# Copying the second quarter of the expert rows behind the state-space tile loads

## The chip, the cores and the metric

The kernel runs on one core of a Trainium2 chip. The metric is the device time of one execution in microseconds (us). The core has five engines that run side by side: TensorE (PE: matrix products and transposes), VectorE (DVE), ScalarE (ACT), GpSimd (POOL) and SyncE (SP), which here only issues DMA transfers. Every engine works through its own instructions in order and waits on semaphores. The transfers that SP issues are listed as queue q1 in the profile and are moved by 16 DMA engines.

## The reference

One token block of 512 positions (and 256 context positions) with 1024 channels goes through two models. The first has two layers, the second ends in a product-key expert layer:

```python
def first_block(...):                      # two layers, l = 0 and 1
    # l = 0: latent attention and retention, joined by w_out
    o_c, o_l = mla_retention_mixer(h_c, h_l, ...)
    x = x + mod_l[:, 2] * o_l
    x = x + mod_l[:, 5] * squared_relu_mlp(h_l, mlp_w1[l], mlp_w2[l])
    # l = 1: a diagonal state-space model in both directions, then a gated unit
    o_c, o_l = s5_mixer(h_c, h_l, p_f, p_b, d_skip, w_glu, need_ctx)
    ...                                    # and the second perceptron

def peer_ffn(h, wq, subkeys, u_tab, v_tab):     # u_tab, v_tab: 16384 rows of 1024 floats each
    ...                                    # 128 rows of each table are chosen for every token
    act = jax.nn.gelu(jnp.einsum('phkd,pd->phk', u_tab[ib], tb)) * gb
    return jnp.einsum('phk,phkd->pd', act, v_tab[ib])
```

All numbers are 32-bit floats.

## The kernel before

The program is one long list of instructions for each engine. Its stages follow one another on TensorE: attention (to about 330 us), retention with its input and output projections (to 680 us), the first perceptron (to 1352 us), the state-space layer (1370 to 1585 us), its gated unit and the second perceptron (to about 1885 us), and then the second model with the expert rows (to 3895 us).

**The expert tables.** For the second half of the tokens the kernel gathers the u row and the v row of an expert in one indirect transfer, from a DRAM tensor `expert_rows` whose row is the two rows side by side (8 KB). That tensor is made during the run from the two tables: `keep_rows(sp, a, which)` (L1218) issues one transfer from DRAM to DRAM for each table, 512 rows of 4 KB, 2048 KB each; in `expert_rows` such a row of 4 KB stands 8 KB behind the last. Rows 0 to 8191 are copied during the first perceptron, two transfers behind each weight block and its two kept pieces (L959, L968 and L977). Rows 8192 to 12287 are copied in one run of 16 transfers behind the load of `w_out` in the retention stage (L1298 and L1299). The last 4096 are copied in the second perceptron, one transfer behind each weight block (L970 and L979). The first gather waits until all 64 are done (L1528), at about 3217 us.

**The state-space stage.** Its matrices were made by GpSimd during the first perceptron and put in DRAM (`s5_store`). Eight tiles i = 0 to 7 are worked through, and for each SP issues three loads: F (`tile_F`, 1024 KB, L1312) and the table (`tile_tab`, 768 KB, L1313), which count on the same semaphore `s5_F`, and E (`tile_E`, 1024 KB, L1316). Each has two buffers. F and the table of tile i wait until TensorE has done `mm1` of tile i-2 and VectorE has turned its states; E of tile i waits for `y` of tile i-2 (L1315). Behind E of tiles 1, 3 and 5 the four weight blocks `xkv` of the memory attention are loaded (2048 KB each: two, one, one; L1318). SP issues in this order, so F of tile i+1 stands behind E of tile i and, for odd i, behind a weight block.

TensorE's order is that of `s5_order()`: for tile i the products `y` (L3152 and L3157), then for tile i+2 the transposes `ta` (L3102), `fa` (L3120) and `tb` (L3113), then `yb` (L3166) of tile i and `fi0` (L3131), `fb` (L3120 again), `mm0` (L3142), `fi1` of tile i+1, one piece of the memory's projections (L3074 or L3081), and `mm1`. `fa` waits for F and the table of its tile, `mm0` for E. ScalarE copies what `fa` makes (L1793) and what `tb` makes (L1797 and L1798) out of the banks, in this order; `fi0` waits for these.

**Behind the stage.** When all pieces of the memory's projection are out of their banks, SP stores them (`kv_kept`, L1322), waits until that has landed, loads the two weight blocks `ada1_4` and then the gated unit's weights. TensorE's next work (L745) needs `ada1_4`.

Of the kernel before, what the change touches and what calls it, by code (L numbers as in the profile page):

```python
# [558 lines left out]
def build(nc, I, consts, out):  # L559

    ctx = ExitStack()
    with ctx:
# [5 lines left out]
        def S(name):  # L568

            if name not in sems:  # L570
                sems[name] = ctx.enter_context(nc.semaphore(name))
            return sems[name]
# [34 lines left out]
        def filled(eng, t, extra=0):  # L607

            eng.wait_ge(S(f"bank{bank_of[t]}_full"), use_of[t] + 1 + extra)
            return ps[bank_of[t]]  # L610
# [34 lines left out]
        def load_block(eng, b, src, extra=0):  # L645


            before = [c for c in range(b) if slot_of[c] == slot_of[b]] or [c for c in range(b) if (slot_of[b], slot_of[c]) in ((NSLOT, 2), (NSLOT + 1, 3))]
            if before:
                filled(eng, last_use[before[-1]], extra)  # L650
            n = 1
            for s in src.shape[1:]:
                n *= s
            dst = ring_part[slot_of[b]][0:src.shape[0], 0:n]
            if len(src.shape) == 3:
                dst = dst.rearrange("p (a b) -> p a b", a=src.shape[1])
            if len(src.shape) == 4:
                dst = dst.rearrange("p (a b c) -> p a b c", a=src.shape[1], b=src.shape[2])
            eng.dma_start(dst, src).then_inc(S(f"weights{slot_of[b]}"), 16)
# [52 lines left out]
        for _i, _vec in enumerate((VEC_A, VEC_B, VEC_C)):  # L712
            _n = sum(v.shape[0] for _, v in _vec)
            vec_rows.append((at(6 * D + _i * P, P), _vec, _n))
            vec_cols.append(sb(f"vec_cols{_i}", [P, _n]))
            _r = 0
            for _name, _v in _vec:
                col_of[_name] = (_i, _r)
                _r += _v.shape[0]

        def col(name, j=0, n=1):

            i, r = col_of[name]
            return vec_cols[i][:, r + j:r + j + n]

        ACT_VECS = [n for _, v, _ in vec_rows for n, _ in v][::2]
        SMALL_LOADS = sum(len(v) for _, v, _ in vec_rows) + 2 - len(ACT_VECS)
        dve_step, act_step, pool_step = Steps("dve_done"), Steps("act_done"), Steps("pool_done")
        silu_c = sb("silu_c", [P, KD, 2])
# [5 lines left out]
        def ada_load(sp, b, l, q):  # L735
            for j in range(2):
                load_block(sp, b + j, ada_w[l][:, :, (2 * q + j) * 512:(2 * q + j + 1) * 512])
# [480 lines left out]
        def keep_rows(sp, a, which):  # L1218

            for w in which:  # L1220
                sp.dma_start(expert_rows[bass.ds(a, 512), w * D:(w + 1) * D], (I["peer_u_2"], I["peer_v_2"])[w][0][bass.ds(a, 512), :])\
                  .then_inc(S("rows_kept"), 16)
# [51 lines left out]
        def _(sp):  # L1274
# [20 lines left out]
                             I["s5_w_glu"][0].rearrange("(k p) n -> p k n", p=P)[:, :, 256 * b:256 * b + 256]).then_inc(S("weights_kept"), 16)  # L1295
            for j in range(2):
                load_block(sp, block0["w_out"] + j, I["w_out"][0].rearrange("(k p) n -> p k n", p=P)[:, :, j * 512:(j + 1) * 512])
            for j in range(8):  # L1298
                keep_rows(sp, 8192 + 512 * j, (0, 1))  # L1299
            ada_load(sp, block0["ada1_2"], 1, 2)  # L1300
            mlp_loads(sp, 0)
            ada_load(sp, block0["ada1_3"], 1, 3)
# [5 lines left out]
            for i in range(S5_TILES):  # L1308
                if i >= 2:
                    filled(sp, ticket0[f"s5_mm1{i - 2}"] + 1)  # L1310
                    sp.wait_ge(S("s5_turned"), 2 * (i - 2) + 2)
                sp.dma_start(tile_F[i % 2], s5_store[i, :, 0:2048]).then_inc(S(f"s5_F{i % 2}"), 16)  # L1312
                sp.dma_start(tile_tab[i % 2], s5_store[i, :, 4096:5632]).then_inc(S(f"s5_F{i % 2}"), 16)  # L1313
                if i >= 2:
                    filled(sp, ticket0[f"s5_y{i - 2}"] + 1)  # L1315
                sp.dma_start(tile_E[i % 2], s5_store[i, :, 2048:4096]).then_inc(S(f"s5_E{i % 2}"), 16)  # L1316
                for j in {1: (0, 1), 3: (2,), 5: (3,)}.get(i, ()):
                    load_block(sp, block0["xkv"] + j, w_kv[:, :, 512 * j:512 * j + 512])  # L1318
            for n in range(8):
# [2200 lines left out]
```

## Time and profile before

| | us |
|---|---|
| median of 3 runs | 3904.86 (3902.64 to 3905.81) |
| the profiled execution | 3898.42, its span 3895.5 |
| PE busy in the span | 3408.8 (88%) |
| DVE, ACT, POOL busy | 1983.0 (51%), 935.9 (24%), 1110.5 (29%) |
| copies into `expert_rows` from SP | 64 transfers of 2048 KB, 20.4 (u) and 21.9 (v) from issue to landing (median) |
| mean granted clock of TensorE | 0.94 |

The profile gives, for one execution, the busy time of the engines, the chain of work that ended last (each step followed back to what released it), groups of instructions with what they waited for, and for a transfer the time from its issue to its landing. TensorE's granted clock is 1.00 (2.4 GHz) or 0.50 (1.2 GHz) of full speed.

### The profile page before, as it was taken

How to read it: one execution, taken by the hardware profiler on the slowest of the kernel's cores; microseconds unless marked ns; L12 is line 12 of the kernel's file. 1: busy time of each engine (PE TensorE's matmuls, PEld its weight loads, DVE VectorE, ACT ScalarE, POOL GpSimd, SP SyncE). 2: the span in 40 equal slices, each digit the busy share in tenths (PEclk: the TensorE clock that was granted, in tenths of full speed). 3: DMA queues.
4: the chain of work that ended last, by engine and by line, in shares of the span. 5: the costliest groups of instructions: out<-in, count | busy, mean ns of one | idle time of the engine just before them, and what ended most of it. 6: DMA issues, size and time to landing. Idle time of an engine off the chain costs nothing.

```text
span 3895.5 us, 47385 instructions
## 1 busy us (share of the span) xinstructions
PE 3408.8 (88%) x17855; PEld 2216.6 (57%) x17855; DVE 1983.0 (51%) x4548; ACT 935.9 (24%) x2125; POOL 1110.5 (29%) x1281
## 2 busy tenths in 40 slices
PE   7999999999999999999989999998687897555655
PEld 4566545555555578788878887765455543111111
DVE  3341263733222388311363257787787436676764
ACT  4352033200000122110342221125423222212212
POOL 1000003262233100000000136654657663333432
PEclk9999999999999999999999999999798999877687
DMA  4439985997785333699322369998879999999998
GB/s 181 149 132 311 322 284 126 317 315 228 246 250 162 124 141 123 219 374 329 121 87 76 125 264 404 413 399 311 307 240 372 392 396 392 421 421 392 421 421 343
DMA packets 337275, 1076.47 MB, mean 276 GB/s; under 512 B 22728, under 2 KB 101012, under 8 KB 292148
## 3 DMA queue, kind: packets, MB, share of 16 engines
q1 hardware_dynamic: 222688, 508.04, 38.2%
q0 software_dynamic: 113968, 565.16, 37.0%
q8 instruction: 125, 2.05, 0.2%
q10 hardware_dynamic: 420, 0.62, 0.1%
q14 instruction: 74, 0.61, 0.0%
HBM read 1045.43 MB, written 236.98 MB: 329 GB/s over the span
## 4 chain that ended last, share of the span: by engine, by line
PE 66%; DVE 15%; DMA 10%; ACT 5%; issue 3%; another core or an unknown queue 1%; POOL 0%; SPq 0%; DVEq 0%; ACTq 0%; POOLq 0%
PE bank L1004 23%; PE bank L3248 9%; PE bank L3474 5%; DMA arena<-expert_rows,arena 4%; DVE ring L2757 4%; DMA ring<-expert_rows,arena 4%; PE bank L2981 3%; PE bank L3215 3%; PE bank L3047 2%; PE bank L3178 1%; DVE arena L2757 1%; DVE arena L2651 1%; PE bank L2857 1%; DMA arena<-in_peer_v,arena 1%; PE bank L2973 1%
## 5 line engine op out<-in xcount | busy, mean ns | idle before, releaser
L3474 PE MATMUL bank<-arena 64*64 64x512 f32 x2520 | 399.4, 704 | 133.0 <-ACT arena L2032 116.3
L1004 PE MATMUL bank<-hT,ring 128*128 128x256 f32 (+1 forms) x1536 | 443.7, 451 | 2.2 <-ACT hT L888 1.7
L1004 PE MATMUL bank<-arena,ring 128*128 128x256 f32 (+1 forms) x1536 | 442.1, 450 | 0.0
L1004 PEld LDWEIGHTS bank<-hT,ring 128*128 128x128 f32 x1536 | 291.1, 190 | 153.5 <-issue 120.3
L3248 PE MATMUL bank<-hT,ring 128*128 128x256 f32 x1536 | 360.8, 393 | 19.8 <-DVE hT L2473 13.1
L1004 PEld LDWEIGHTS bank<-arena,ring 128*128 128x128 f32 x1536 | 291.8, 190 | 148.9 <-issue 121.5
L3474 PE MATMUL bank<-ring,arena 64*64 64x512 f32 x1256 | 239.0, 785 | 138.2 <-ACT arena L2032 137.7
L3248 PEld LDWEIGHTS bank<-hT,ring 128*128 128x128 f32 x1536 | 297.8, 197 | 85.1 <-issue 37.1
L1520 POOL DMA_INDIRECT ring<-in_peer_u,arena x256 | 277.4, 1084 | 208.8 <-DVE ring L2757 94.6
L1562 POOL DMA_INDIRECT arena<-in_peer_v,arena x240 | 276.6, 1153 | 180.8 <-PE bank L3474 62.5
L2757 DVE SCALAR_TENSOR_TENSOR ring<-ring,xT 128x1024 f32<-128x1024 f32 x256 | 309.0, 1220 | 22.8 <-DMA ring<-in_peer_u,arena 17.4
L3474 PEld LDWEIGHTS bank<-arena 64*64 64x64 f32 x2520 | 100.9, 150 | 348.2 <-ACT arena L2032 169.7
L2032 ACT ACTIVATE arena<-arena,rstd 128x64 f32<-128x64 f32 x472 | 141.3, 339 | 421.5 <-DVE rstd L2803 398.5
L2757 DVE SCALAR_TENSOR_TENSOR ring<-ring,bank 128x1024 f32<-128x1024 f32 x141 | 171.7, 1220 | 103.7 <-DMA ring<-expert_rows,arena 101.9
L3474 PEld LDWEIGHTS bank<-ring,arena 64*64 64x64 f32 x1256 | 57.2, 160 | 284.3 <-ACT arena L2032 215.4
L1036 DVE SCALAR_TENSOR_TENSOR xT<-bank,modT,xT 128x512 f32<-128x512 f32 (+1 forms) x96 | 54.8, 573 | 316.6 <-PE bank L1004 316.4
L1016 ACT ACTIVATE arena<-bank 128x512 f32<-128x512 f32 (+1 forms) x96 | 43.5, 454 | 712.5 <-PE bank L1004 712.4
L799 POOL TENSOR_TENSOR hT<-hT 128x256 f32<-128x256 f32 (+1 forms) x30 | 34.7, 1156 | 581.5 <-ACT hT L1937 261.1
L1539 POOL DMA_INDIRECT ring<-expert_rows,arena x141 | 133.5, 947 | 232.6 <-PE bank L3474 200.6
L1028 DVE TENSOR_TENSOR arena<-arena 128x512 f32<-128x512 f32 (+1 forms) x96 | 55.7, 589 | 276.5 <-ACT arena L1016 275.7
L2757 DVE SCALAR_TENSOR_TENSOR arena<-arena,bank 128x1024 f32<-128x1024 f32 x115 | 140.2, 1220 | 75.0 <-DMA arena<-expert_rows,arena 73.5
L1539 POOL DMA_INDIRECT arena<-expert_rows,arena x115 | 108.7, 945 | 179.0 <-PE bank L3474 154.2
(601 smaller groups left out, 5348.0 us busy)
## 6 DMA issues: line engine op xcount, KB each, us to landing
expert_rows<-in_peer_u SPq DMA_DIRECT2D x32, 2048.0 KB, 20.4
expert_rows<-in_peer_v SPq DMA_DIRECT2D x32, 2048.0 KB, 21.9
ring<-in_mlp_w SPq DMA_DIRECT2D x32, 2048.0 KB, 11.2
ring<-in_ada_w SPq DMA_DIRECT2D x24, 2048.0 KB, 10.5
late_weights<-in_mlp_w SPq DMA_DIRECT2D x32, 1024.0 KB, 14.4
ring<-late_weights SPq DMA_DIRECT2D x32, 1024.0 KB
ring<-weights_kept SPq DMA_DIRECT2D x32, 1024.0 KB
s_store<-arena POOLq DMA_DIRECT2D x8, 2816.0 KB, 9.8
```

Of the source, the lines that this page charges most:

```text
L1004: last = pe.matmul(bank[:, 0:hi - lo], w[:, k, m * P:(m + 1) * P], x[:, k, lo:hi], start=(k == 0), stop=(k == 7))
L1028: dve.tensor_tensor(hid[:, m, lo:hi], hid[:, m, lo:hi], hid[:, m, lo:hi], ALU.mult)\
L1520: pool.indirect_dma_start(u_row[u % ERING], None, I["peer_u_2"][0], bass.IndirectOffsetOnAxis(idxs[:, u // EXPERTS, u % EXPERTS:u % EXPERT ...
L1539: pool.indirect_dma_start(both_rows[i % F_SLOTS], None, expert_rows, bass.IndirectOffsetOnAxis(idxs[:, u // EXPERTS, u % EXPERTS:u % EXPER ...
L1562: pool.indirect_dma_start(v_row[v_slot(v)], None, I["peer_v_2"][0], bass.IndirectOffsetOnAxis(idxs[:, v // EXPERTS, v % EXPERTS:v % EXPERT ...
L2032: act.activation(diag[:, d % V_SLOTS, :], eye2, ACT.Copy, scale=acts[:, d % (AGROUP * ACT_GROUPS):d % (AGROUP * ACT_GROUPS) + 1]).then_inc ...
L2757: dve.scalar_tensor_tensor(row, row, 1.0, h_tok[u // EXPERTS], ALU.mult, ALU.mult, accum_out=dots[:, u % 64:u % 64 + 1]).then_inc(S("u_use ...
L2981: last = pe.matmul(bank[:, 0:hi - lo], w[:, k, m * P:(m + 1) * P], hT[:, k, lo:hi], start=(k == 0), stop=(k == KD - 1))
L3047: last = pe.matmul(bank[:, 0:hi - lo], w[:, k, m * P:(m + 1) * P], mixT[:, k, lo:hi], start=(k == 0), stop=(k == 7))
L3215: last = pe.matmul(bank[:, 0:HALF], w[:, k, n % 2 * P:n % 2 * P + P], y, start=(k == 0), stop=(k == KD - 1))
L3248: last = pe.matmul(bank[:, first:first + HALF], w[:, k, c:c + P], y, start=(k == 0), stop=(k == KD - 1))
L3474: last = pe.matmul(banks[2 * r + n][QUADS[r if y == 0 else 1 - r], :], diag[QUADS[r], (v + y) % V_SLOTS, :], v_part(v + y)[QUADS[r], 512 * ...
```

## The change

The run of 16 copies leaves the retention stage. In the state-space stage each tile's loads are followed by the two copies of 512 rows. Same transfers, same bytes, the same semaphore; nothing is added to a wait.

```diff
@@ sync engine, behind the loads of w_out
             for j in range(2):
                 load_block(sp, block0["w_out"] + j, I["w_out"][0].rearrange("(k p) n -> p k n", p=P)[:, :, j * 512:(j + 1) * 512])
-            for j in range(8):
-                keep_rows(sp, 8192 + 512 * j, (0, 1))
             ada_load(sp, block0["ada1_2"], 1, 2)
@@ sync engine, loop over the state-space tiles
                 if i >= 2:
                     filled(sp, ticket0[f"s5_y{i - 2}"] + 1)
                 sp.dma_start(tile_E[i % 2], s5_store[i, :, 2048:4096]).then_inc(S(f"s5_E{i % 2}"), 16)
+                keep_rows(sp, 8192 + 512 * i, (0, 1))
                 for j in {1: (0, 1), 3: (2,), 5: (3,)}.get(i, ()):
                     load_block(sp, block0["xkv"] + j, w_kv[:, :, 512 * j:512 * j + 512])
```

SyncE in the retention stage, the change against the kernel before. The rows with a minus are the first two of 16 copies of `keep_rows`; `in_ada_w` is the load of `ada1_2`:

```order
 L1294 DMA gate_weights<-in_s_w_glu 1024x1x256 x8
 L659 DMA ring<-in_w_out 128x8x512 x2
-L1221 DMA expert_rows<-in_peer_u 512x1024
-L1221 DMA expert_rows<-in_peer_v 512x1024
...
 L659 DMA ring<-in_ada_w 128x8x512 x2
 L659 DMA ring<-in_mlp_w 128x8x512
```

The load of `ada1_2` now stands directly behind `w_out`.

SyncE in the state-space stage before, tiles 3 and 4: F, the table and E of tile 3, the third `xkv` block, then tile 4.

```order
L1312 DMA arena<-s5_store 128x2048
L1313 DMA arena<-s5_store 128x1536
L1316 DMA arena<-s5_store 128x2048
L659 DMA ring<-in_xattn_wkv_2 128x8x512
L1312 DMA arena<-s5_store 128x2048
L1313 DMA arena<-s5_store 128x1536
L1316 DMA arena<-s5_store 128x2048
```

The same place after the change:

```order
L1310 DMA arena<-s5_store 128x2048
L1311 DMA arena<-s5_store 128x1536
L1314 DMA arena<-s5_store 128x2048
L1221 DMA expert_rows<-in_peer_u_2 512x1024
L1221 DMA expert_rows<-in_peer_v_2 512x1024
L659 DMA ring<-in_xattn_wkv_2 128x8x512
L1310 DMA arena<-s5_store 128x2048
L1311 DMA arena<-s5_store 128x1536
L1314 DMA arena<-s5_store 128x2048
```

Two copies of 2048 KB now stand between E of a tile and everything that SP issues next: for tile 3 that is the weight block and then F and the table of tile 4.

## Rows read from the trace of the kernel before

**Rows 1.** Chain of work that ended last, whole span: start, duration, what.

```profile
465.59 41.29 PE bank L2981 x128
692.05 660.04 PE bank L1004 x2044
```

**Rows 2.** SyncE's timeline, retention stage: start, duration, what was issued.

```profile
442.09 3.60 SPq L1221 DMA_DIRECT2D expert_rows<-in_peer_u  x1
544.22 19.75 SPq L659 DMA_DIRECT2D ring<-in_ada_w  x2
```

**Rows 3.** TensorE's timeline, state-space stage; brackets: idle before, and its releaser.

```profile
1447.36 1.04 PE L3120 MATMUL bank<-ident,arena 128*128 128x128 f32 x8
1473.09 1.04 PE L3120 MATMUL bank<-ident,arena 128*128 128x128 f32 x8
1474.44 0.85 PE L3113 MATMUL bank<-ident,arena 96*128 96x96 f32 x8 [0.31 <-ACT arena L1785]
1478.92 2.06 PE L3142 MATMUL bank<-arena 64*128 64x128 f32 x32
1524.56 1.04 PE L3120 MATMUL bank<-ident,arena 128*128 128x128 f32 x8
```

**Rows 4.** SyncE's timeline, state-space stage.

```profile
1421.73 0.43 SPq L1313 DMA_DIRECT2D arena<-s_store  x1
1448.00 0.65 SPq L1313 DMA_DIRECT2D arena<-s_store  x1
1472.28 0.32 SPq L1316 DMA_DIRECT2D arena<-s_store  x1
1499.47 0.76 SPq L1313 DMA_DIRECT2D arena<-s_store  x1
```

**Rows 5.** Issue to landing (last number, us): tables of tiles 3, 4, 6.

```profile
arena<-s_store SPq DMA_DIRECT2D x1, 768.0 KB, 8.4
...
arena<-s_store SPq DMA_DIRECT2D x1, 768.0 KB, 14.4
...
arena<-s_store SPq DMA_DIRECT2D x1, 768.0 KB, 14.3
```

**Rows 6.** Windows, perceptron one: engines' busy us, clock, DMA share, GB/s.

```profile
940.00:952.00 12.00, 12.00 (x37) 6.81 (x36) 3.06 (x6) 0.00 (x0) 0.00 (x0) 1.00 1.00 351
952.00:968.00 16.00, 16.00 (x50) 9.20 (x49) 8.43 (x13) 0.00 (x0) 0.00 (x0) 1.00 1.00 259
```

**Rows 7.** SyncE's timeline, perceptron two.

```profile
1776.21 0.38 SPq L659 DMA_DIRECT2D ring<-in_mlp_w  x1
1776.85 0.83 SPq L1221 DMA_DIRECT2D expert_rows<-in_peer_v  x1
```

**Rows 8.** Issue to landing of those two.

```profile
ring<-in_mlp_w SPq DMA_DIRECT2D x1, 2048.0 KB, 10.1
expert_rows<-in_peer_v SPq DMA_DIRECT2D x1, 2048.0 KB, 14.7
```

**Rows 9.** SyncE's timeline, end of the state-space stage.

```profile
1549.47 0.32 SPq L1316 DMA_DIRECT2D arena<-s_store  x1
1567.26 0.32 SPq L1322 DMA_DIRECT2D kv_kept<-ring  x1
1575.40 1.01 SPq L659 DMA_DIRECT2D ring<-in_ada_w  x2
```

**Rows 10.** TensorE's timeline, first work behind the stage.

```profile
1589.87 4.90 PE L745 MATMUL bank<-ring,silu_c 128*2 128x256 f32 x64 [4.42 <-issue]
```

**Rows 11.** Issue to landing: E of tile 7, and `kv_kept`.

```profile
arena<-s_store SPq DMA_DIRECT2D x1, 1024.0 KB, 5.3
...
kv_kept<-ring SPq DMA_DIRECT2D x1, 2048.0 KB, 8.1
```

**Rows 12.** Windows around 1370 us, columns as in rows 6.

```profile
1366.40:1370.60 4.20, 0.03 (x1) 0.00 (x0) 3.63 (x8) 4.20 (x9) 0.44 (x2) 1.00 1.05 388
1370.60:1374.00 3.40, 3.04 (x15) 2.98 (x16) 2.65 (x4) 2.00 (x5) 0.61 (x2) 0.50 0.94 343
```

## The prediction

> **What bounds the kernel now.** I read the chain of work that ended last first. In the retention stage and in the first perceptron it is TensorE without a break: one piece of 41.29 us while the 16 copies run, and later one of 660.04 us [rows 1]. SP issues the first copy at 442.09 and gets to the next load, `ada1_2`, at 544.22 [rows 2]. So the copies fill the DMA queue for some 100 us, but no TensorE, VectorE or ScalarE work of the chain waits for a transfer there. In the state-space stage the chain is TensorE and ScalarE in turn, with a period of 25.73 us: `fa` of tile 3 starts at 1447.36, that of tile 4 at 1473.09 [rows 3]. TensorE is idle there for fractions of a microsecond only, so whatever makes `fa` or `mm0` late is added to the end.
>
> The reader should look next at the distance between a load's landing and its use. The table of tile 4 was issued at 1448.00 [rows 4] and landed 14.4 us later [rows 5], at 1462.4; `fa` of tile 4 needs it at 1473.09, 10.7 us later. The table of tile 6: 1499.47 + 14.3 = 1513.8, needed at 1524.56 [rows 3 to 5], 10.8 us. These two stand behind an `xkv` block. The table of tile 3 has no such block ahead: 1421.73 + 8.4 = 1430.1, needed at 1447.36, 17.3 us.
>
> **What goes.** The 16 copies leave the retention stage. Loads behind them on SP come earlier: `ada1_2` is needed only for the perceptron, 100 us and more after it was issued [rows 1, 2], and what follows it waits for free slots. GpSimd's loads have the queue more to themselves, but its products are wanted only at the state-space stage. I take the gain as zero; as the chain has no transfer in this stretch, I see no bound below it except a microsecond or so.
>
> **What comes.** Eight pairs of copies, one behind E of each tile. A later load on the queue is moved back by what a pair takes (p). Three rows give p:
> - Pairs in a long full queue: (544.22 - 442.09) / 16 = 6.38 us for one copy, p = 12.8 [rows 2].
> - A pair in a short burst behind a weight block and its kept pieces, with the queue empty before: between 952 and 968 us 16 us at 259 GB/s, which is 4.14 MB, the pair's 4.19 MB, against 351 GB/s in the 12 us before [rows 6]. p = 16.0.
> - A single copy behind a single weight block: block landed at 1776.21 + 10.1 = 1786.3, copy at 1776.85 + 14.7 = 1791.6 [rows 7, 8], 5.2 us. Two of these would be p = 10.5.
>
> I take 16.0, because the state-space pairs are also u and v back to back, in short bursts behind loads, with an empty queue between. The ends are 10.5 and, as nothing excludes a slower one, some 18.
>
> Tiles 0 and 1: their loads and copies are issued as soon as the perceptron's last block is in use, before the stage begins; two pairs, 32 us, fit ahead of it, and the first `xkv` blocks wait for slots anyway. Hidden. Tile 3: 17.3 us of distance against p = 16.0. Hidden by 1.3 us. Tile 5 has no weight block ahead either, and 5 us more once tile 4 was late. Hidden. E of tile 4 is issued at 1472.28 [rows 4], behind a table that then has just landed; it needs about 3 us of transfer more and is wanted at 1478.92 plus the delay [rows 3]. Hidden.
>
> Tile 4: the pair of tile 3 goes ahead of `xkv`, F and the table. Landing 1462.4 + 16.0 = 1478.4, 5.3 us after `fa` wanted to start. Of these 0.3 us are covered, since `tb` waits 0.31 us for ScalarE anyway [rows 3]: **+5.0 us**. Tile 6 the same way: 1513.8 + 16.0 - 1524.56 = 5.2, less 0.3: **+4.9 us**. The two add up, since SP issues tile 6's loads when `y` of tile 3 is done, which is late by the first delay.
>
> The stage's end: E of tile 7 lands at 1549.47 + 5.3 = 1554.8, and the last pair goes behind it to 1570.8. `kv_kept` is issued at 1567.26 and takes 8.1 us alone [rows 9, 11]; SP waits for it, then loads `ada1_4` at 1575.40, and TensorE stands idle for it for 4.42 us until 1589.87 [rows 9, 10]. So this string of transfers is already on the path. `kv_kept` would move bytes from about 1569; the pair holds them to about 1570.5: **+1.7 us**, and nothing if p is under 14.3.
>
> The clock: after a gap of 4.2 us without TensorE work the granted clock was 0.50 for the next 3.4 us [rows 12]. Such a piece costs at most 1.7 us of TensorE time (an estimate, half of 3.4). Two gaps of about 5 us may bring none, one or two. I take one: **+1.7 us**.
>
> Sum: 5.0 + 4.9 + 1.7 + 1.7 = 13.3 us. The profiled execution was 3898.42 (its span 3895.5), 6.4 under the median 3904.86; I add the sum to the median: **3918 us**, or about 3909 for the span.
>
> As a function of p the sum is 2 (p - 11.0) + (p - 14.3, if positive) + the clock: 3.6 at 12.8, about 7.8 at 14.7, 13.3 at 16.0, 19 at 17.3 with two falls of the clock. A measurement of this kernel tells about 0.2%, 7.8 us, from no change. So p = 14.7 decides between slower and the same.
>
> **The rivals.**
> - The pairs run at p = 11 to 14.7, as in the long queue. Then `fa` of tiles 4 and 6 waits 2 us each: +4, **3909 us**. For it: the same rows 8192 to 12287 made that pace. Against it: that pace is a mean over a full queue, and the short bursts were slower.
> - Hidden anyway, p up to 10.7: +0, **3905 us**. For it: the 5.2 us of the single copy [rows 8]. Against it: no u and v pair in a row went so fast. The Trainium skill's DMA: Bandwidth & Descriptors (section Bandwidth, Measured) says a transfer costs about 2 us fixed plus its bytes at 436 GB/s; by this the pair's bytes would take an estimated 9.6 us, the table of tile 4 would land before `fa`, and the change would cost nothing. The 16 us of rows 6 speak against using it for copies from DRAM to DRAM.
> - Pile-up. From p = 17.3 on the tables of tiles 3 and 5 are late as well. At p = 20: tile 3 by 2.7, tiles 4 and 6 by about 9 each, tile 5 by 3, `kv_kept` by 6, and two or three falls of the clock: +33, **3938 us**. For it: nothing longer than 16 in the rows; the queue would have to be slower when loads and copies are mixed.
> - Faster, because something in the retention stage or GpSimd's preparation was held up by the full queue after all: -9 or more would be needed; the chain shows nothing of the kind. **3895 us**.
>
> The same page (section Latency and other measured facts) reports that copies whose rows lie at large powers of two apart fall to about half rate, and guesses that the DMA engines then run in step on the same memory channel. Our 8 KB spacing is far under the spacings that it lists; if it held here at its 207 GB/s, a pair would take an estimated 20 us, which is the pile-up.
>
> **How the numbers follow.** Forecast (p from 14.7 to 17.3) 0.55; long-queue pace 0.22; hidden 0.10; pile-up 0.10; faster 0.03. Slower by over 0.2%: 0.65. Within: 0.32. Faster: 0.03. The range 3906 to 3926 holds the forecast with its bounds of p and of the clock, and the long-queue case; it leaves out most of the hidden case, the pile-up and the faster one.
>
> **What would show it.** In the profile after: `fa` (L3120) of tiles 4 and 6 with a wait of about 5 us before it that ends with the table's landing, and none of over 1 us at tiles 3, 5 and 7; 10 to 11 us more from `ta` of tile 0 to `yb` of tile 7; pairs that last 16 us in windows of GB/s; the granted clock at 0.50 once or twice between 1475 and 1545; `kv_kept` landing 1 to 2 us later after its issue. No change between 442 and 1350. It is wrong if the pairs take under 14.7 us, if `fa` of tile 3 waits, or if `mm0` does (E late).

## The result, and the profile after

In the session in which both kernels were timed side by side, the changed kernel took 3921.69 us (median of five, 3915.23 to 3925.44) and the kernel before 3902.64 (median of five, 3895.04 to 3905.81). The ratio is 1.0051, 95% interval 1.0038 to 1.0063: slower by 15 to 25 us. The profiled execution of after took 3915.23 us with a span of 3913.2, against 3898.42 and 3895.5 before. It fell a little under its median, as the one of before did.

**Where the time is.** The first line below is of before, the others of after; columns as in [rows 6]. Without the copies the retention stage's transfers fall from 324 to 59 GB/s, and TensorE is busy for the same 121 us of the 123. No time is gained there that these windows show. (What answers to the pair's window in [rows 6] stands with the experiment dense, below.)

```profile
442.00:565.00 123.00, 120.98 (x417) 56.51 (x418) 69.03 (x112) 32.90 (x47) 0.93 (x1) 0.99 1.00 324
```

```profile
442.00:565.00 123.00, 120.99 (x431) 56.56 (x431) 70.92 (x116) 33.69 (x49) 0.93 (x1) 1.00 0.16 59
```

The chain of work that ended last, after (start, duration, what; the longest pieces). The two TensorE pieces of [rows 1] have kept their lengths within 3 us. New are three transfers out of `s_store` in the state-space stage, where before none was in the chain:

```profile
462.37 41.30 PE bank L2980 x128
...
686.04 662.92 PE bank L1004 x2046
1420.57 25.15 DMA arena<-s_store
1460.72 15.84 DMA arena<-s_store
1509.27 27.09 DMA arena<-s_store
```

These are the tables of tiles 3, 4 and 6. TensorE's timeline of after shows what waits for them; the number in brackets is the idle time before, and behind it stands its releaser. The lines answer to [rows 3]; line numbers of after are one or two lower than before's.

```profile
1445.77 1.09 PE L3119 MATMUL bank<-ident,arena 128*128 128x128 f32 x8 [1.19 <-DMA arena<-s_store]
...
1470.20 1.11 PE L3101 MATMUL bank<-ident,hT 128*96 128x128 f32 x8
1476.61 1.97 PE L3119 MATMUL bank<-ident,arena 128*128 128x128 f32 x8 [5.29 <-DMA arena<-s_store]
1478.37 1.49 PE L3112 MATMUL bank<-ident,arena 96*128 96x96 f32 x8
...
1480.82 2.83 PE L3130 MATMUL bank<-arena 128*64 128x96 f32 x32
...
1503.76 1.11 PE L3101 MATMUL bank<-ident,hT 128*96 128x128 f32 x8
1504.71 1.04 PE L3119 MATMUL bank<-ident,arena 128*128 128x128 f32 x8
...
1508.05 1.54 PE L3130 MATMUL bank<-arena 128*64 128x96 f32 x32 [0.50 <-ACT arena L1797]
...
1536.41 1.97 PE L3119 MATMUL bank<-ident,arena 128*128 128x128 f32 x8 [5.80 <-DMA arena<-s_store]
```

Read it in two steps. `fa` (L3119) waits 1.19 us at tile 3, 5.29 at tile 4 and 5.80 at tile 6, and not at tile 5. And behind the two long waits the same work takes nearly twice as long: the eight turns 1.97 us instead of 1.04, the 32 products of L3130 2.83 instead of 1.54. The granted clock says why (windows of after, columns as in [rows 6]; the number ahead of the last two is the clock): 0.50, that is 1.2 of 2.4 GHz. Each of the two pieces at half clock lasted 10.2 us: from 1473.8 to 1484.1, of which 7.4 us hold TensorE's work, and from 1535.3 to 1545.5, of which 9.1 us do. The rest lies in the wait itself.

```profile
1474.00:1484.00 10.00, 7.39 (x58) 6.83 (x59) 1.35 (x2) 2.30 (x6) 0.00 (x0) 0.50 1.03 345
1535.30:1545.50 10.20, 9.09 (x66) 8.20 (x68) 2.95 (x5) 3.01 (x8) 0.00 (x0) 0.50 1.02 330
```

SyncE's timeline of after, tiles 3 and 4 (answers to [rows 4]), shows what the tables stand behind: E of tile 3, the pair of copies (L1221), an `xkv` block, F, and then the table (L1311). SyncE's issue of F is held for 14.54 us.

```profile
1443.60 0.32 SPq L1314 DMA_DIRECT2D arena<-s_store  x1
1443.97 0.53 SPq L1221 DMA_DIRECT2D expert_rows<-in_peer_u  x1
1444.54 0.74 SPq L1221 DMA_DIRECT2D expert_rows<-in_peer_v  x1
1445.32 0.71 SPq L659 DMA_DIRECT2D ring<-in_xattn_wkv  x1
1446.14 14.54 SPq L1310 DMA_DIRECT2D arena<-s_store  x1
1460.72 1.13 SPq L1311 DMA_DIRECT2D arena<-s_store  x1
```

Issue to landing (last number, us), from the DMA view of after: E of tile 3, then u, v and the table of tile 4.

```profile
arena<-s_store SPq DMA_DIRECT2D x1, 1024.0 KB, 5.4
...
expert_rows<-in_peer_u SPq DMA_DIRECT2D x1, 2048.0 KB, 14.9
...
expert_rows<-in_peer_v SPq DMA_DIRECT2D x1, 2048.0 KB, 21.6
...
arena<-s_store SPq DMA_DIRECT2D x1, 768.0 KB, 15.8
```

E landed at 1443.60 + 5.4 = 1449.0, v at 1444.54 + 21.6 = 1466.1: the pair had the queue for 17.1 us. The table landed at 1460.72 + 15.8 = 1476.5, and `fa` starts at 1476.61.

The end of the stage (SyncE's timeline, then TensorE's first work behind it; answers to [rows 9, 10]). From `kv_kept`'s issue to SyncE's next one it is 9.9 us, against 8.1 before.

```profile
1564.45 0.32 SPq L1314 DMA_DIRECT2D arena<-s_store  x1
...
1582.24 0.33 SPq L1321 DMA_DIRECT2D kv_kept<-ring  x1
1592.14 1.01 SPq L659 DMA_DIRECT2D ring<-in_ada_w  x2
```

```profile
1606.79 5.36 PE L745 MATMUL bank<-ring,silu_c 128*2 128x256 f32 x64 [6.38 <-issue]
```

**The sum.** I take the time from `ta` of tile 0 to the first product of the gated unit: 229.75 us before (1370.96 to 1600.71), 249.80 after (1367.83 to 1617.63), 20.05 more. The rest of the span behind it is 2294.8 and 2295.6 us. Between the `ta` of one tile and the next it is 25.73 us wherever nothing waits; from tile 7's `ta` to the first product it is 51.37 before. After has 26.74 at tile 3 (+1.0), 33.56 at tile 4 (+7.8), 25.73 at tile 5, 34.83 at tile 6 (+9.1) and 53.31 at the end (+1.9): 19.8 of the 20.05 us. The span of after is only 17.7 us longer, because its stage begins 3.1 us earlier; whether that is a gain of the change is taken up with both_places.

### The profile page after: what moved, and what is told of

The parts are those of the page before. It is cut to its first block, busy times and chain, and to the rows that moved or that the text cites. A ratio compares the mean times of both kernels' runs of the same rounds, so it can differ in the third digit from the quotient of the medians.

```text
span 3913.2 us, 47385 instructions
## 1 busy us (share of the span) xinstructions
PE 3415.6 (87%) x17855; PEld 2223.2 (57%) x17855; DVE 1981.6 (51%) x4548; ACT 937.1 (24%) x2125; POOL 1111.0 (28%) x1281
## 4 chain that ended last, share of the span: by engine, by line
PE 64%; DVE 13%; DMA 12%; ACT 4%; issue 3%; another core or an unknown queue 1%; POOL 1%; SPq 0%; DVEq 0%; ACTq 0%; POOLq 0%
PE bank L1004 23%; PE bank L3247 9%; PE bank L3473 6%; DMA arena<-expert_rows,arena 4%; DMA ring<-expert_rows,arena 4%; PE bank L3214 4%; DVE ring L2756 3%; PE bank L2980 3%; DMA arena<-s_store 2%; PE bank L3046 2%; PE bank L3177 1%; PE bank L2856 1%; PE bank L745 1%; DMA ring<-in_ada_w 1%; DMA arena<-in_peer_v,arena 1%
## 5 line engine op out<-in xcount | busy, mean ns | idle before, releaser
L3247 PE MATMUL bank<-hT,ring 128*128 128x256 f32 x1536 | 357.3, 390 | 17.4 <-DVE hT L2472 10.6
```

The source lines that it names most:

```text
L3247: last = pe.matmul(bank[:, first:first + HALF], w[:, k, c:c + P], y, start=(k == 0), stop=(k == KD - 1))
```

## Experiments

Every kernel was timed beside the kernel before on the same chip (whose medians there were 3902.8, 3903.8 and 3905.9 us). The table gives its ratio to that and, from its own trace, the times just used. p is the time by which the copies delay the next table: from E's issue to the table's landing, less the same in before.

| kernel | ratio, 95% interval | tile 3 | tile 4 | tile 6 | end | stage | p, tables of tiles 3 to 7 |
|---|---|---|---|---|---|---|---|
| before | 1 | 25.73 | 25.73 | 25.73 | 51.37 | 229.8 | |
| after | 1.0051 [1.0038, 1.0063] | 26.74 | 33.56 | 34.83 | 53.31 | 249.8 | 18.5, 17.1, 15.7, 16.7, 18.3 |
| both_places | 1.0057 [1.0037, 1.0078] | 26.21 | 34.35 | 35.56 | 52.27 | 251.0 | 18.1, 16.5, 16.6, 17.2, 18.4 |
| only_3_5 | 1.0055 [1.0038, 1.0072] | 25.73 | 36.42 | 35.88 | 52.05 | 251.1 | 18.0 and 17.8 (tiles 4, 6) |
| not_3_5_7 | 1.0006 [0.9997, 1.0016] | 26.49 | 25.74 | 25.73 | 51.76 | 231.3 | 18.3, 16.7, 17.8 (tiles 3, 5, 7) |
| one_table | 1.0046 [1.0029, 1.0062] | 25.73 | 30.98 | 32.91 | 52.25 | 244.2 | 17.0, 15.2, 14.8, 14.9, 16.1 |
| u_only | 1.0006 [0.9995, 1.0017] | 25.73 | 25.73 | 25.73 | 52.36 | 230.8 | 10.0, 8.9, 8.0, 7.8, 9.3 |
| dense | 1.0007 [0.9996, 1.0018] | 25.73 | 27.10 | 27.31 | 51.85 | 234.4 | 12.4, 12.3, 11.9, 12.6, 13.6 |
| behind_table | 1.0017 [1.0007, 1.0027] | 25.74 | 27.88 | 29.41 | 51.53 | 235.8 | |
| awake | 1.0059 [1.0042, 1.0076] | 27.11 | 35.15 | 36.04 | 52.63 | 253.3 | |
| awake_half | 1.0031 [1.0020, 1.0042] | 26.04 | 34.69 | 31.60 | 52.22 | 246.8 | 17.8, 17.9, 17.8, 16.9, 18.0 |
| awake_mid | 1.0043 [1.0028, 1.0059] | 26.35 | 31.58 | 32.76 | 53.00 | 244.7 | 18.1, 17.4, 16.4, 18.0, 19.5 |

The stage's figure is from one profiled execution each. It holds the time of tile 0, which went from 22.8 to 24.4 us between these traces with no relation to the copies that I can see, so differences of under 2 us in it say nothing; the columns of single tiles are finer. The ratio is coarser: its interval is 7 to 16 us wide.

### Was anything gained in the retention stage?

**both_places**: the copies of before stay where they were, and the same source rows are copied once more in the state-space stage, into a spare tensor of the same layout. In this diff and the others `-` and `+` are against the changed kernel.

```diff
+        spare_rows = nc.dram_tensor("spare_rows", (4096, 2 * D), F32).ap()
...
+            for j in range(8):
+                keep_rows(sp, 8192 + 512 * j, (0, 1))
...
-                keep_rows(sp, 8192 + 512 * i, (0, 1))
+                for w in range(2):
+                    sp.dma_start(spare_rows[bass.ds(512 * i, 512), w * D:(w + 1) * D], (I["peer_u_2"], I["peer_v_2"])[w][0][bass.ds(8192 + 512 * i, 512), :])\
+                      .then_inc(S("spare"), 16)
```

> The kernel before, with the 16 copies kept in the retention stage, and the same 16 copies done once more in the state-space stage at the places of the change, into a spare tensor that nobody reads. Theory: the copies in the retention stage cost the chain nothing, so this is the changed kernel in time: 20 us above before, waits of 1, 5 and 6 us before fa of tiles 3, 4 and 6. Rival: taking the copies out of the retention stage gave something back that hid a larger loss; then this is more than 22 us above before.

Measured: 3920.27 us, ratio 1.0057, as after (1.0051). The stage takes 251.0 us, again with waits of 0.67, 5.22 and 6.31 us at tiles 3, 4 and 6. The two ratios alone leave several microseconds open. The traces leave less: `ta` of tile 0 starts between 1366.3 and 1373.4 us (mean 1369.7) in the six kernels with none of the 16 copies in the retention stage, and between 1366.3 and 1371.0 (mean 1369.3) in the three that have all of them. What the copies cost in the retention stage doesn't show above that spread, and the 3.1 us by which the stage of after begins earlier than that of before lie within it. The loss is in the state-space stage.

### Which pairs cost?

**only_3_5**: only the pairs behind E of tiles 3 and 5 are in the state-space stage, the others are where they were before.

```diff
+            for j in (0, 1, 2, 4, 6, 7):
+                keep_rows(sp, 8192 + 512 * j, (0, 1))
...
-                keep_rows(sp, 8192 + 512 * i, (0, 1))
+                if i in (3, 5):
+                    keep_rows(sp, 8192 + 512 * i, (0, 1))
```

> Only the pairs of tiles 3 and 5 are behind their E; the six others stay in the retention stage. Theory: the loss sits at the two tables that stand behind a pair and a weight block: 7.8 and 9.1 us with their pieces of half clock, so 16 to 17 us above before with a quarter of the copies moved; no wait before fa of tile 3. Rival: the queue is full over the whole stage and each pair pays its share; then a quarter of the pairs costs a quarter, 5 us.

Measured: 3923.69 us, ratio 1.0055. A quarter of the copies makes the whole loss: 21.3 us in the stage, where 16 to 17 were expected. TensorE's timeline shows the two waits, both longer than in after. At tile 4 it is 2.0 us more. Half of that is a larger p (18.0 against 17.1); the other half is that in after tile 3 was late by 1.0 us, so that tile 4 wanted its table that much later, and here no such delay comes ahead. At tile 6 the 1.1 us more are all from p (17.8 against 16.7). The pieces at half clock are 13.65 us long.

```profile
1480.64 1.97 PE L3122 MATMUL bank<-ident,arena 128*128 128x128 f32 x8 [7.27 <-DMA arena<-s_store]
...
1542.42 1.97 PE L3122 MATMUL bank<-ident,arena 128*128 128x128 f32 x8 [6.89 <-DMA arena<-s_store]
```

**not_3_5_7**: the reverse. Pairs 3, 5 and 7 are in the retention stage, the other five behind their E.

```diff
+            for j in (3, 5, 7):
+                keep_rows(sp, 8192 + 512 * j, (0, 1))
...
-                keep_rows(sp, 8192 + 512 * i, (0, 1))
+                if i not in (3, 5, 7):
+                    keep_rows(sp, 8192 + 512 * i, (0, 1))
```

> The pairs of tiles 0, 1, 2, 4 and 6 are behind their E, those of tiles 3, 5 and 7 stay in the retention stage. Theory: a pair costs only where a weight block stands between it and the next table (tiles 3 and 5) or where kv_kept comes behind it (tile 7). Here only fa of tile 3 waits, by 1 us: 1 us above before, and no half clock in the stage. Rival: the queue's load counts, not the place; five eighths of the copies cost 12 us.

Measured: 3905.95 us, ratio 1.0006 [0.9997, 1.0016], not told from before. The pairs are as slow as ever (p 18.3, 16.7, 17.8), yet the waits for tables 3, 5 and 7 are only 0.86, 0.51 and 0.42 us, and tiles 4 and 6 wait for none. The two kernels together say that what costs is not how many bytes are moved in this stage but which load stands behind them, and how much room that load had.

### Why does a pair take 17 us?

**one_table**: each pair is two copies from the same table (u for tiles 0 to 3, v for 4 to 7) instead of u and v into alternate halves of the same rows.

```diff
-                keep_rows(sp, 8192 + 512 * i, (0, 1))
+                for part in range(2):
+                    keep_rows(sp, 8192 + 1024 * (i % 4) + 512 * part, (i // 4,))
```

> The changed kernel, but the two copies behind each tile's E are of the same table: 1024 rows of u behind each of tiles 0 to 3, 1024 rows of v behind each of tiles 4 to 7. Same bytes in the same places of the queue. Theory A: a pair takes 17 us because a u copy and the v copy of the same rows overlap on the DMA engines and write next to each other; two copies of one table then take about 12 us, the table of tile 4 lands about 0 to 1 us late, and the whole is 0 to 4 us above before. Rival B: 17 us is what 4 MB from DRAM to DRAM take in a short burst behind loads, whichever table: 20 us above before, as the changed kernel.

Measured: 3917.12 us, ratio 1.0046, p 14.8 to 17.0, in the mean 15.6 against 17.3 in after. That u and v go to neighbouring addresses at the same time is worth 0.9 to 2.2 us of a pair, in the mean 1.7, and not the 5 of the first theory, which fell. The rival was nearer, but not met in full either: the stage is some 14 us above before, not 20.

**dense**: as both_places, but the spare tensor holds each table's rows of 4 KB one behind the other. In `expert_rows` (and in both_places) they stand 8 KB apart.

```diff
+        spare_rows = nc.dram_tensor("spare_rows", (2, 4096, D), F32).ap()
...
+            for j in range(8):
+                keep_rows(sp, 8192 + 512 * j, (0, 1))
...
-                keep_rows(sp, 8192 + 512 * i, (0, 1))
+                for w in range(2):
+                    sp.dma_start(spare_rows[w, bass.ds(512 * i, 512), :], (I["peer_u_2"], I["peer_v_2"])[w][0][bass.ds(8192 + 512 * i, 512), :])\
+                      .then_inc(S("spare"), 16)
```

> As both_places (16 copies in the retention stage, and once more in the state-space stage into a spare tensor), but the spare tensor keeps u and v apart, so that its rows of 4 KB stand directly behind one another instead of 8 KB apart. Theory: the pair is slow (17 us) because of the spacing of its target rows; then a pair takes 10 to 12 us, no table is late by over 1 us, and the time is that of before, within 4 us. Rival: the spacing has no part in it; 20 us above before and tables late by 5 to 6 us, as in both_places.

Measured: 3908.68 us, ratio 1.0007. p fell to about 12.5, the waits of tiles 4 and 6 to 1.54 and 1.76 us (at most 1 was expected), and the clock stayed at 1.00 behind both waits. For the pair of tile 3, after has E landed at 1449.0 and v at 1466.1, 17.1 us later; dense has E at 1448.0 and v at 1460.1 (issued at 1443.96, landed 16.1 us later), so 12.0 us. The windows below, first of after, then of dense (last number: GB/s), start with the pair in both. That of after lies within the pair; that of dense holds 5 us of the `xkv` block as well, so its 333 GB/s are not the pair's alone:

```profile
1449.00:1465.00 16.00, 16.00 (x184) 14.08 (x181) 14.10 (x30) 1.85 (x4) 0.00 (x0) 1.00 1.03 251
```

```profile
1449.00:1465.00 16.00, 16.00 (x170) 13.85 (x169) 15.07 (x30) 1.85 (x4) 0.00 (x0) 1.00 0.96 333
```

So the layout of the target makes the pair slow. It differs from both_places in two things: each table's rows stand behind one another, and u and v no longer go to neighbouring addresses. By one_table the second is worth some 1.7 us; that leaves some 3 of the 4.8 us (mean p 17.4 in both_places, 12.6 in dense) for the spacing of the rows, if the two add up, which no run tested. The Trainium skill's DMA: Bandwidth & Descriptors (section Latency and other measured facts) has copies between DRAM tensors with rows 512 KiB apart at 207 GB/s, hardly under the 214 that it calls full, and at 103, about half, only from 4 MiB on. Here a spacing of 8 KB came with a slower pair, 17.1 us against 12.0; by what mechanism, no run here shows.

The layout isn't all of it. The 16 copies of before have that same spacing, and in the long queue they were faster. The first landed at 442.09 + 22.0 = 464.1, the last at 536.15 + 31.0 = 567.2: 15 copies in 103.1 us, 13.7 us for a pair. The windows of before (columns as in [rows 6]) show that this pace, too, began slowly:

```profile
462.00:470.00 8.00, 8.00 (x20) 3.61 (x19) 7.72 (x13) 0.00 (x0) 0.00 (x0) 1.00 1.02 265
...
490.00:500.00 10.00, 10.00 (x33) 6.00 (x32) 0.00 (x0) 0.98 (x2) 0.00 (x0) 1.00 1.03 332
```

A short burst would then always be in the slow part. That is argued from these rows; no run tested it.

**u_only**: only the copies of u are behind the tiles, those of v in the retention stage.

```diff
+            for j in range(8):
+                keep_rows(sp, 8192 + 512 * j, (1,))
...
-                keep_rows(sp, 8192 + 512 * i, (0, 1))
+                keep_rows(sp, 8192 + 512 * i, (0,))
```

> Behind each tile's E only the copy of u; the eight copies of v stay in the retention stage. Theory: a table behind one copy lands 6 to 10 us later than before, under the 10.7 us that it has, so fa waits nowhere and the time is that of before, 0 to 2 us above. Rival: any copy behind E costs; half the copies cost half, 10 us.

Measured: 3904.62 us, ratio 1.0006. One copy displaces the table by 7.8 to 10.0 us, half a pair and not the 5.2 us of [rows 7, 8]. That is under the 10.7 us of room that tiles 4 and 6 have, and there is no wait on a table anywhere. The end costs 1.0 us, of which 0.3 is a wait of tile 7's `mm0` for E.

### Place in the queue, or presence in the stage?

**behind_table**: all eight pairs stay in the stage, but each goes behind the tile's F and table and ahead of its E.

```diff
                 sp.dma_start(tile_tab[i % 2], s5_store[i, :, 4096:5632]).then_inc(S(f"s5_F{i % 2}"), 16)
+                keep_rows(sp, 8192 + 512 * i, (0, 1))
...
                 sp.dma_start(tile_E[i % 2], s5_store[i, :, 2048:4096]).then_inc(S(f"s5_E{i % 2}"), 16)
-                keep_rows(sp, 8192 + 512 * i, (0, 1))
```

> The changed kernel with the pair of copies issued behind each tile's forward matrices and table, ahead of the tile's E matrices, in place of behind E. All copies are still there, and no copy stands any more between an E and the next table. Theory (a pair holds up by some 17 us whatever is queued next on SyncE's queue, and the cost is what that is late beyond its cover): no wait of the turns (L3119) on the table at any tile and no piece at half clock behind them; E is issued 26 to 34 us ahead of its use and lands 5 to 9 us behind its issue now, so with 17 us more it comes up to 4 us late behind tiles whose E is issued late: waits of 0 to 4 us on E at L3141 in at most four tiles; the last table and kv_kept have no copy between them but E7's, so the end stays within 0.5 us of 51.4 or pays up to 2. Stage 230 to 240 us against 249.8 after and 229.8 before; time 3903 to 3912 us. Rival (the copies cost by their mere presence in this stage, through the shared memory, wherever they stand): the stage stays above 244 us and the time above 3915 us.

Measured: 3913.08 us, ratio 1.0017 [1.0007, 1.0027], clearly under after's 1.0051 [1.0038, 1.0063], and a stage of 235.8 us (the time is 1 us above the expected range, the stage in it). No turn waits for a table. The wait has moved to `mm0`, for E, at tiles 4 and 6:

```profile
1483.41 2.06 PE L3141 MATMUL bank<-arena 64*128 64x128 f32 x32 [2.08 <-DMA arena<-s_store]
...
1537.05 3.56 PE L3141 MATMUL bank<-arena 64*128 64x128 f32 x32 [2.10 <-DMA arena<-s_store]
```

Of 20 us, 14 are gone by position alone. The rival, that the copies cost by being there, falls. E of tile 4 was issued at 1474.61 and landed 8.8 us later, at 1483.4, where `mm0` starts. At tile 6 a piece of 3.4 us at half clock began at 1536.8, in the gap ahead of `mm0`; the 32 products take 3.56 us instead of 2.06. At tile 4, behind a gap of the same length, the clock stayed at 1.00. Still, the place in the retention stage is better, as nothing waits there at all.

### What does the clock cost?

**awake**: products whose result nobody reads fill TensorE's gaps ahead of the turns of tiles 3, 4 and 6. They add work and take none out.

```diff
+                    if step == "fa" and i in (3, 4, 6):
+                        stay_awake(pe, t0, {3: 8, 4: 44, 6: 48}[i])
```

> The changed kernel, with TensorE doing 8, 44 and 48 extra small products (they go nowhere) just before it waits for the tables of tiles 3, 4 and 6. Theory: the state-space stage lost 19.9 us, of which some 12 are waits for the tables (1.2, 5.3 and 5.8 us at tiles 3, 4 and 6) and some 6.4 are TensorE at half clock behind the two long waits (the granted clock was 0.50 for 10.2 us twice). With the extra products the clock stays at 1.00 there and the periods of tiles 4 and 6 shrink by 2.8 and 3.6 us: 13 to 14 us above the kernel before. Rival: the periods are long because the late table also delays VectorE and ScalarE; then the clock changes nothing and it stays at 20 us above before, or more, since the extra products take time.

Measured: 3923.76 us, ratio 1.0059. There was no wait for a table and no half clock behind one any more, but the fill itself was too long. Each call counts double, 88 products at tile 4 (TensorE's timeline):

```profile
1478.08 9.99 PE L813 MATMUL bank<-ident 128*128 128x128 f32 x88
```

Those 9.99 us are longer than the gap of 5.3 they were to fill. So the time of this run tells nothing of the clock's price, since the fill set the end.

**awake_half** and **awake_mid**: the same with less fill, at tiles 4 and 6 only. 42 and 46 products in the first, 56 and 46 in the second.

```diff
+                    if step == "fa" and i in (4, 6):
+                        stay_awake(pe, t0, {4: 21, 6: 23}[i])
```

```diff
+                    if step == "fa" and i in (4, 6):
+                        stay_awake(pe, t0, {4: 28, 6: 23}[i])
```

> The run awake had extra products of twice the wait: 44 of them took 10 us, not 5, and kept TensorE from the landed table. Here 21 and 23 of them, some 4.8 and 5.2 us, fill the waits of 5.3 and 5.8 us before fa of tiles 4 and 6. Theory: 2.8 and 3.6 us of the two long periods are the half clock; with it gone the periods are 30.8 and 31.3 us instead of 33.6 and 34.8, and the whole 13 to 14 us above before. Rival: the clock falls anyway or costs nothing there; the periods stay at 33.6 and 34.8.

> The changed kernel with 56 spare products ahead of tile 4's turns (42 in the run before) and 46 ahead of tile 6's, as there. They write a bank that nothing reads; the output is unchanged. There, tile 4's 42 products took 4.85 us, 2.01 us of waiting were left, and a piece of 6.8 us at half clock came behind it (period 34.69 us); at tile 6, 0.93 us were left and no half clock came (31.60 us). Theory (half clock comes behind a gap of TensorE, and costs some 3 us each time): at tile 4 less than 1 us of waiting is left, no piece at half clock, and the period falls to that of a wait alone, 25.7 + 6 to 7 = 31.5 to 32.7 us; tile 6 again 31 to 32 us; the stage 244 to 246 us against 249.8. Rival (tile 4's half clock has another cause, such as the transfers): the period of tile 4 stays at 34 to 35 us with a piece at half clock though the wait is gone. Time 3912 to 3917 us by the theory, 3915 to 3920 by the rival: the trace decides, not the time.

Measured: awake_half 3915.90 us (1.0031), awake_mid 3918.58 us (1.0043). In awake_half 2.01 us of waiting were left at tile 4, a piece of 6.8 us at half clock came with it, and the tile took 34.69 us, as the rival had it. At tile 6 0.93 us were left, no half clock came, and it took 31.60 us instead of 34.83, as the theory had it. In awake_mid the fill is long enough at tile 4 as well (its timeline):

```profile
1471.51 6.42 PE L813 MATMUL bank<-ident 128*128 128x128 f32 x56
1477.76 1.04 PE L3121 MATMUL bank<-ident,arena 128*128 128x128 f32 x8
...
1480.69 1.54 PE L3132 MATMUL bank<-arena 128*64 128x96 f32 x32 [0.59 <-ACT arena L1797]
...
1536.20 1.09 PE L3121 MATMUL bank<-ident,arena 128*128 128x128 f32 x8 [2.08 <-DMA arena<-s_store]
```

The turns are back to 1.04 us and L3132 to 1.54, against 1.97 and 2.83 in after. The tables are no earlier (p 17.4 and 18.0), and tiles 4 and 6 take 31.58 and 32.76 us: 2.0 and 2.1 us less than in after, though the table of tile 6 was 1.3 us later by p. That rules out the rival, by which tile 4 was to stay at 34 to 35 us. The periods still hold the tables' delay, which is larger here: from `ta` to `fa` it is 7.2 and 8.3 us, against 6.4 and 6.9 in after. The price of the clock can be read behind it. From the start of `fa` to that of `mm0` tiles 4 and 6 take 5.42 and 5.48 us in awake_mid, 5.42 at both in awake, and 5.48 behind the wait of tile 4 in dense and behind the wait of tile 3 in after; with the half clock, in after, they take 8.20 and 8.87. So the half clock cost 2.7 and 3.4 us there, 0.1 more at tile 6's `mm0`, and some 6.2 in sum.

The times are no witness: 3918.58 lies in the range of the rival (3915 to 3920) and not in that of the theory (3912 to 3917). The ratios agree in direction with less than after, but their intervals overlap, so only the traces show this.

## Why the prediction was right, point by point

Sign, mechanism and places were right: 3918 us were forecast, and 3921.69 came. The two are nearer than the forecast deserves. It stood on a median of 3904.86 for before, and beside after that kernel took 3902.64; the loss is 19.0 us (15 to 25 by the interval), and 13.3 were forecast. In the trace it is 19.8. Four terms were too small, and none was too large.

- **Retention gain zero.** Right as far as can be told, by both_places, by the starts of the stage given there, and by the two lines of 442 to 565.
- **p = 16.0.** Measured 15.7 to 18.5, mean 17.3, which was the upper edge of the forecast's own bounds. Of the three rows the one nearest to this case, the short burst of [rows 6], was the right choice and still 1.3 us low. Why it was low the runs don't show; they show that p goes with the target's layout (about 12.5 in dense). The single copy's 5.2 us [rows 7, 8] is far from u_only's 7.8 to 10.0. And the long queue's 12.8 was misread: it took SyncE's issues, while the queue was still filling, for landings, which give 13.7.
- **Tile 3 "hidden by 1.3 us".** Wrong. Its p was 18.5 against 17.3 of room, so 1.2 us were to be expected, and 1.19 us of wait came (+1.0 on the period). The prediction named this as a sign of error, and it is one, in p. In a second sign, 10 to 11 us more from `ta` of tile 0 to `yb` of tile 7, 18.1 came.
- **Tile 4, +5.0.** Waited 5.29 us, 5.0 after the 0.31 us which it would wait anyway. This hit is partly luck: p was 1.1 us higher, but the delay of tile 3 covered 1.0 of it. In only_3_5, without that delay and with a p of 18.0, the wait was 7.27.
- **Tile 6, +4.9.** Waited 5.80, so 5.5.
- **`kv_kept`, +1.7.** The end was 1.9 us longer. The mechanism held: SyncE's next issue came 9.9 instead of 8.1 us behind. The size is not firm: in the other five kernels with all eight spaced pairs behind E the end was 0.9 to 1.6 us longer than before.
- **The clock, +1.7.** This is the step that failed most. The periods of tiles 4 and 6 grew by 7.8 and 9.1 us, of which waiting explains 5.0 and 5.5. 2.8 and 3.6 us are left, together 6.4, and the stretch from `fa` to `mm0` shows 6.2 of them directly. The prediction took one piece of 3.4 us, from [rows 12]; there were two, each of 10.2 us. The price by half of the work at half clock held as an upper bound (7.4 and 9.1 us of it cost 2.7 and 3.5); the number and the length of the pieces were wrong. The trace of before had a longer piece to offer, 6.8 us, which began in the gap of 4.42 us of [rows 10]:

```profile
1585.60:1592.40 6.80, 2.53 (x26) 0.88 (x30) 1.94 (x2) 5.38 (x17) 0.00 (x0) 0.50 1.05 386
```

- **Hidden rest.** Tile 5 had no wait, and `mm0` none on E. Both right in after. Tile 5 owes it to tile 4's delay: its room in before is 1498.82 - 1482.85 = 15.97 us, which the prediction didn't work out, and in not_3_5_7, where nothing is late ahead of it, it waited 0.51. And `mm0` of tile 7 waited 0.2 to 0.7 us for E in one_table, u_only, dense and the three awake runs.

1.0 for tile 3, 0.6 for tile 6, 0.2 for `kv_kept` and 4.7 for the clock make 6.5, the difference between 13.3 and 19.8. The prediction's own formula gives 19 us at the measured p of 17.3 with two falls of the clock. That is near by luck: it has 6.3 us for each of the tiles 4 and 6 and 3.0 for `kv_kept`, more than came, and 3.4 for the clock and nothing for tile 3, less than came.

Of the rivals, the long-queue pace is what dense shows (p about 12.5): it waits 1.54 and 1.76 us, and its time is 1.0007 of before. "Hidden anyway" is what u_only shows. The pile-up began, in that tile 3 was late, but tile 5 was not. The estimate of 9.6 us for a pair, from the Trainium skill's DMA: Bandwidth & Descriptors, was low even for dense rows (12.0 measured). Its formula stands in that page's section Anatomy of one DMA and was fitted to transfers that GpSimd issues, not to copies that SyncE issues. The estimate of 20 us for spaced rows was high (17.1). It was also misread: 207 GB/s is the page's rate at a spacing of 512 KiB and no halved rate. Here the measurements decide.

## What to carry to other kernels

A copy that nobody waits for is free only if what is queued behind it has room; measure the distance from a load's landing to its use for every load of the stage, and put copies where everything that follows them on the queue has much room, or where the chain holds no transfer. Here 10.7 us of room held one copy (8 to 10 us) but not two (17 us). When a wait of some 5 us is added to TensorE, add to it 1.1 to 3.7 us for the work at half clock behind it (what waits of 4.1 to 7.3 us brought here; the more usual price was 2.7 to 3.7), and take a copy's pace from a row with the same target layout and the same length of burst.

## What was not expected of the hardware

- Copies of 4 KB rows, from DRAM to DRAM, into rows 8 KB apart: 17.1 us for 4.19 MB (251 GB/s in a window within the pair) against 12.0 us into contiguous rows of two separate regions. Some 1.7 us of the difference go with u and v being written side by side; what is left over is put down to the spacing.
- The same spaced copies made 13.7 us for a pair in a queue of 16. Their window was at 265 GB/s at the start and at 332 later. Why is open.
- SyncE's issue of a load can be held for 14.5 us when a pair and a weight block are ahead of it. By itself it seems to cost nothing: p is 17.1 us at tile 4 with it and 18.5 at tile 3, where no issue was held. No run tested it.
- Idle gaps of TensorE of 5.3 and 5.8 us (after) came with 10.2 us at 0.50 of the clock, gaps of 7.3 and 6.9 us (only_3_5) and 6.3 us (both_places) with 13.65 us, and gaps of 4.4 and 4.1 us (one_table) with 3.4 and 10.2 us. The clock fell within the gap, so that part of the piece cost nothing. Waits of 1.54 and 1.76 us (dense) and 2.08 us (behind_table, and awake_mid behind 46 spare products) had none; one of 2.10 us (behind_table) had 3.4 us, and one of 2.01 us behind 42 spare products 6.8 us. The length of the gap alone doesn't tell.
